# One layer with 32 routed experts on one core: TensorE reads an item's two table words inside the item ahead, and the body for one block comes first

## What is computed

```python
def expert_block(args):
    e, tok, gt = args
    xb = xf[tok]
    gu = xb @ w_gu[e] + b_gu[e]
    gate, up = gu[:, :D_EXPERT], gu[:, D_EXPERT:]
    gate = jnp.minimum(gate, SWIGLU_LIMIT)
    up = jnp.clip(up, -SWIGLU_LIMIT, SWIGLU_LIMIT)
    h = (up + 1.0) * gate * jax.nn.sigmoid(SWIGLU_ALPHA * gate)
    y = h @ w_down[e] + b_down[e]
    return y * gt[:, None].astype(y.dtype)
```

## Time and profile before

| | us |
|---|---|
| median of 3 runs | 2352.89 (2351.8 to 2353.47) |
| the profiled execution | 2354.07 |
| its span, first to last instruction | 2352.3 |
| PE busy | 2243.4 (95%) |
| DVE busy | 1712.5 (73%) |
| ACT busy | 1341.7 (57%) |

### The profile page before, as it was taken

One profiled execution on the slowest core, in us unless ns is written; L12 is line 12 of the kernel. 1 busy time (PEld: TensorE's weight loads), 2 busy tenths in 40 slices (PEclk: granted clock), 3 DMA queues, 4 the chain that ended last, 5 costly groups with the idle time before them and its releaser, 6 DMA issues.

```text
span 2352.3 us, 35229 instructions
## 1 busy us (share of the span) xinstructions
PE 2243.4 (95%) x10483; PEld 1658.5 (71%) x10484; DVE 1712.5 (73%) x2828; ACT 1341.7 (57%) x1785; POOL 359.4 (15%) x231
## 2 busy tenths in 40 slices
PE   8999998889999999999999999999999999999992
PEld 3544446667755678877787877878787787887872
DVE  0387794745445667778978799787979979778797
ACT  0368723555312555656766577566757757556575
POOL 0000941200020210101201031021103103101030
PEclk9999998989999999999999999999999999999996
DMA  4100002000322967688988799797979979768795
GB/s 179 72 5 36 1 0 92 1 1 1 135 79 99 279 212 233 229 307 291 339 300 303 238 328 370 230 324 236 373 232 335 365 231 343 284 230 307 231 335 216
DMA packets 83741, 494.13 MB, mean 210 GB/s; under 512 B 13342, under 2 KB 14622, under 8 KB 32580
## 3 DMA queue, kind: packets, MB, share of 16 engines
q1 hardware_dynamic: 69408, 451.24, 52.3%
q0 software_dynamic: 12592, 38.82, 6.8%
q10 hardware_dynamic: 1686, 3.38, 0.4%
HBM read 462.97 MB, written 38.01 MB: 213 GB/s over the span
## 4 chain that ended last, share of the span: by engine, by line
PE 76%; DVE 9%; issue 8%; ACT 5%; DVEq 1%; DMA 1%; ACTq 0%; POOL 0%; POOLq 0%; SPq 0%
PE ps L912 10%; PE ps L910 10%; PE ps L911 10%; PE ps L581 6%; PE ps L907 6%; PE ps L908 6%; PE ps L592 5%; PE ps L772 5%; DVE wlo L1630 3%; ACT whi L1158 2%; PE ps L755 2%; PE ps L920 2%; PE ps L736 2%; PE ps L875 1%; PE ps L743 1%
## 5 line engine op out<-in xcount | busy, mean ns | idle before, releaser
L1630 DVE TENSOR_TENSOR wlo<-raw,whi 128x2048 fp32r<-128x2048 f32 x388 | 886.1, 2288 | 244.5 <-ACT whi L1158 207.8
L1158 ACT ACTIVATE whi<-raw 128x2048 fp32r<-128x2048 f32 x388 | 743.2, 1916 | 327.4 <-PE ps L912 326.2
L911 PE MATMUL ps<-wlo,xhi 128*128 128x512 f32 x1024 | 398.8, 389 | 0.0
L912 PE MATMUL ps<-whi,xlo 128*128 128x512 f32 x1024 | 398.8, 389 | 0.0
L910 PE MATMUL ps<-whi,xhi 128*128 128x512 f32 x1024 | 398.7, 389 | 0.0
L1963 POOL DMA_INDIRECT acc<-ysb,idx_cur x45 | 87.5, 1945 | 959.5 <-DVE ysb L1797 584.4
L912 PEld LDWEIGHTS ps<-whi,xlo 128*128 128x128 f32 x1024 | 192.3, 188 | 40.3
L911 PEld LDWEIGHTS ps<-wlo,xhi 128*128 128x128 f32 x1024 | 192.2, 188 | 40.1
L910 PEld LDWEIGHTS ps<-whi,xhi 128*128 128x128 f32 x1024 | 192.3, 188 | 38.9
L910 PE MATMUL ps<-whi,hhi 128*128 128x512 f32 x512 | 206.5, 403 | 0.0
L912 PE MATMUL ps<-whi,hlo 128*128 128x512 f32 x512 | 200.4, 391 | 0.0
(11 more groups left out here) (340 smaller groups left out, 3346.9 us busy)
## 6 DMA issues: line engine op xcount, KB each, us to landing
raw<-in_w_gu SPq DMA_DIRECT2D x260, 1024.0 KB, 6.8
raw<-in_w_dn SPq DMA_DIRECT2D x128, 1024.0 KB, 5.6
raw<-in_w_out SPq DMA_DIRECT2D x2, 2048.0 KB, 12.5
h1all<-in_x SPq DMA_DIRECT2D x4, 1024.0 KB, 8.5
hext<-h1all SPq DMA_DIRECT2D x8, 512.0 KB, 3.1
acc<-h1all SPq DMA_DIRECT2D x8, 512.0 KB, 3.8
fin<-acc SPq DMA_DIRECT2D x4, 1024.0 KB, 8.3
out<-fin SPq DMA_DIRECT2D x8, 512.0 KB, 2.6
```

The source lines that it names most:

```text
L911: pe.matmul(bank_ap, hi, wlo[slot][:, col, :], start=False, stop=False)
L912: return pe.matmul(bank_ap, lo, whi[slot][:, col, :], start=False, stop=stop)
L1158: act.activation(whi[j % 2][:, 4 * g:4 * g + 4, :], raw[:, (j + 2) % 3, 4 * g:4 * g + 4, :], ACT.Copy)\
L1630: dve.tensor_tensor(wlo[j % 2][:, s, :], raw[:, (j + 2) % 3, s, :], whi[j % 2][:, s, :].bitcast(f32), ALU.subtract).then_inc(lo_done, 1)
```

## The change

Three things change, all on PE. The helper `load_entries` reads the two words into two registers that last over the turns, without the bounds check that `entry` makes; it is called once ahead of the loop for item 0, and in every item between `gate_up(1)` and `gate_up(2)` for the item after. The head of a turn only copies the two registers. And the body for one block stands ahead of the body for two.

```diff
-            entry = item_table(pe)
 ...
+            next_b1, next_n1 = pe.alloc_register("next_b1"), pe.alloc_register("next_n1")
+
+            def load_entries(i):
+
+                pe.reg_load(next_b1, table[0:1, bass.ds(i + MAX_ITEMS, 1)])
+                pe.reg_load(next_n1, table[0:1, bass.ds(i + 2 * MAX_ITEMS, 1)])
+
             def item(i, n1, blocks):
                 gate_up(0, i, n1, blocks)
                 find_slots(i + 1, fills_before(i, 0) + 1)
                 gate_up(1, i, n1, blocks)
+                load_entries(i + 1)
                 gate_up(2, i, n1, blocks)
 ...
             pe.wait_ge(tail_const, 8)
+            load_entries(0)
             with pe.Fori(0, n_items) as i:
-                b1, n1 = entry(1, i, 1), entry(2, i, MAX_ITEMS)
+                b1 = pe.snap(next_b1, min_val=0, max_val=1)
+                n1 = pe.snap(next_n1, min_val=0, max_val=MAX_ITEMS)
+                with pe.If(b1 < 1):
+                    item(i, n1, (0,))
                 with pe.If(b1 > 0):
                     item(i, n1, (1, 0))
-                with pe.If(b1 < 1):
-                    item(i, n1, (0,))
```

## The result

The changed kernel takes 2340.94 us, median of 4 runs (2335.43 to 2342.44), beside 2353.18 for the kernel before (4 runs, 2351.8 to 2353.99). The ratio is 0.994, 95% interval 0.9927 to 0.9952. It is faster, by 12.2 us; 2342.2 was forecast.

What follows compares the result with a forecast made beforehand. PE, busy 95% of the span, was taken as the bound, with DVE next in one-block items. Removing 18 border stalls wins 8.5 + 2.2 = 10.7 us, giving 2342.2 us; the 8-in-10 range was 2336 to 2350.

Steps and rivals of the forecast that it cites:

- The stalls' cause: Behind one-block items PE's sequencer needs about 2.65 us at the border, queued matmuls cover 1.67; moving two reads ends 18 stalls.
- The price of a read, 0.7 us: Each table read with its register work at PE's loop head was taken to cost 0.7 us, from DVE's border.
- The mid-item reads at 0: Two reads between quarters 1 and 2 cost 0, hidden behind twelve queued matmuls, 2.7 us of cover against 1.4.
- From one block to two: 9 x 0.94 = 8.5 us: Nine borders into two-block items each win 0.72 us of stall and 0.22 of pipeline refill, 8.5 us in all.
- the refill: A two-block item without a stall ahead need not refill the pipeline and runs 0.22 us shorter, 59.97 against 60.19.
- From one block to one: 9 x 0.24 = 2.2 us: Of the 0.98 us stall, 0.74 returns as PE waits for DVE's chain at `turn_h(3)`; 0.24 stays, nine times.
- The first turn at 0: The stall at the first item's end moves ahead of item 0 and costs the same: 0, bounds -5 to +3.5 us.
- The sum: 8.5 + 2.2 = 10.7 us won over the whole kernel, giving 2342.2 us against 2352.89, -0.45%.
- Cheap reads: Rival, 15%: PE's border is jumps and register work; at 0.25 us a read, stalls into two blocks stay, 2350.7 us.
- The gain used up: Rival, 12%: another chain of one-block items, or a second 3.5 us code stall in the first turn, leaves 2350 us.
- A stop in mid-item: Rival, 7%: the mid-item reads stop the array, 0.7 us in each of 32 items, slower at 2364.6 us.
- No give-back: Rival, 8%: DVE's border catches up and one-block items win the whole 0.98 + 0.2 us; 19.1 us won, 2333.8.

Runs made afterwards that it cites:

- reads_only: The changed kernel with the bounds check kept and the two-block body put first again, PE's reads still in mid-item: 2340.51 us, ratio 0.9944 to the kernel before.
- order_only: The kernel before with only the two bodies exchanged, PE's reads left at the loop's head: 2356.31 us, ratio 1.0011.
- head_reads_live: The kernel before with four more bounds-checked table reads at PE's loop head, which stay in the program: 2436.0 us in one run beside 2353.54.
- mid_reads_live: guarded with six more bounds-checked table reads in mid-item on PE, eight in all, which stay in the program: 2414.78 us in one run beside 2353.54.
- dve_ahead: guarded with DVE's four table reads also moved ahead, one behind each of four wlo splits of an item: 2329.95 us, ratio 0.990 to the kernel before.
- head_reads: The kernel before with four more reads at PE's loop head into an unused register, which the compiled program leaves out: 2352.14 us in one run.
- dve_only: The kernel before with DVE's four reads moved ahead and PE's left at its head: 2349.45 us beside 2353.83, ratio 0.9976.
- guarded: The changed kernel with the bounds check on PE's mid-item reads kept, and a register move added: 2340.93 us, ratio 0.9944 to the kernel before.
- mid_reads: guarded with six more mid-item reads on PE into an unused register, which the compiled program leaves out: 2340.75 us in one run.

## Why the prediction was right, step by step

**The stalls' cause.** Right. The reads' move alone ended all 18 (reads_only), the exchange of bodies none (order_only).

**The price of a read, 0.7 us.** Measured 0.64 (head_reads_live). Needed were 0.61 from one block to two, and the prediction called that close. It was closer than it sounded: 1.29 taken out against 1.28 to be taken. That these nine stalls went whole, and not all but a few hundredths, is in part luck. The price of a jump with its compare, 0.25, measured 0.28 (order_only). Its 2.40 us into a two-block item begin at this row, which the earlier trace rows do not show, and end at 1193.97:

```profile
1191.56 0.44 PE L888 MATMUL ps<-consts,xg_all 128*128 128x128 f32 x2 [0.23 <-DVE xlo L1748]
```

**The mid-item reads at 0.** Right, and the cover of 2.7 us was near: an estimated 3.4 in most items, 1.9 to 2.8 in one-block items behind two blocks (mid_reads_live). Eight reads, an estimated 5.15 us, were more than it could hide, and showed 1.7 to 3.3 us. That the queue is deep was taken from the border behind a two-block item, an estimated 2.9 us of work without a gap. How deep it is no run shows, for a wait of PE can end the cover first; the measured cover decides.

**From one block to two: 9 x 0.94 = 8.5 us.** Measured 9 x 0.82 = 7.4. The gap's part was right (0.72). The part for the refill was set at 0.22 from one pair of items; the 1018.86 item of the earlier trace rows, 59.96 to its last matmul, is the longest of nine whose mean is 59.90. Over all nine it is 0.10. The mean of the nine, against 59.75 for an item without a stall, would have given 0.15, and 7.8 us in all.

**From one block to one: 9 x 0.24 = 2.2 us.** The mechanism was right: of a gap of 0.97 most is given back to DVE's chain, and `turn_h(3)` came at +27.54 in the item laid out above, for +27.49. The step named one of the chain's two places only: in that item more of the delay is taken at `turn_h(2)` (0.53 us over the usual distance) than at `turn_h(3)` (0.27). The items vary, 37.29 to 38.19 to their last matmul where 37.79 was forecast, with a mean of 37.69. That makes 3.0 us. dve_ahead showed the cause: with DVE's four reads out of its border, L875 no longer waits, and these items are 36.90 long. What makes one such item 0.9 us longer than another is not shown.

**The first turn at 0.** Wrong by 2.0 us in the profiled execution. It was taken that the stall, the 3.71 us at item 0's end, moves ahead of item 0 and costs the same. No run shows this 0 or its bounds of -5 and +3.5, which were the author's estimates; before the change the stall and the eight matmuls behind it, starting 0.20 further apart than usual at a granted clock of 0.51, come to 5.1 us (3.5 + 1.6), and 2.0 of them were won. The stall moved into item 0, between its two blocks' quarter 0, and from item 0's start to item 2's the loop took 2.6 us less. Of that, 1.1 us is a shorter stall (2.62 for 3.71) and 1.6 the eight matmuls at half the clock that no longer follow it. In the table "half" counts the matmuls of the stretch that start about 0.43 apart, at a granted clock of 0.50 or 0.51 where a stretch of such alone was read (793 to 799 us in reads_only, 858.7 to 862 before; it is 1.00 from 795.7 to 799 us in the changed kernel, where they start 0.23 apart), and "stall" is the longest distance between two starts:

| profiled execution | PE's reads | body first | item 0's start to item 2's, us | stall | half |
|---|---|---|---|---|---|
| before | head | two-block | 125.30 | 3.71 | 8 |
| head_reads (the same program) | head | two-block | 125.21 | 3.52 | 8 |
| dve_only | head | two-block | 126.79 | 3.56 | 16 |
| order_only | head | one-block | 122.24 | 2.34 | 0 |
| reads_only | mid-item | two-block | 124.93 | 2.07 | 14 |
| after | mid-item | one-block | 122.67 | 2.62 | 0 |
| guarded | mid-item | one-block | 122.71 | 1.38 | 7 |
| mid_reads (guarded again) | mid-item | one-block | 123.04 | 1.61 | 7 |
| dve_ahead | mid-item | one-block | 123.24 | 1.67 | 7 |

The body order is shown to set where the stall falls: at item 0's end with the two-block body first, inside item 0 with the other. With the reads at the head the exchange also shortens the stretch, by 3.0 to 4.6 us, in one execution against three. With the reads in mid-item the stretch is 1.7 to 2.3 us shorter, but that is not shown to come from the order: in reads_only the 14 matmuls at half the clock, an estimated 2.8 us (14 x 0.20), stand at item 0's start, far ahead of the stall, and without them its stretch is no longer than the others. In guarded, mid_reads and dve_ahead the seven slow matmuls come just ahead of the stall, which is then shorter than in the changed kernel. Why the stall's length changes, and what decides between the two clock levels here, is open: the start of item 0 itself lies between 790.7 and 795.9 us from one profiled execution to the next, and the fetches were not varied by themselves.

**The sum.** 10.7 us were forecast and 11.6 measured between the profiled executions, 12.2 between the medians. The terms are 7.4 for 8.5, 3.0 for 2.2, 2.0 for 0, and -0.7 behind the last matmul, which no step spoke of and which was not followed up. So the sum is nearer than its parts, which is luck: the first turn made up for the refill.

**The two parts of the change.** The exchange of bodies, which the forecast took as neutral in the first turn and dear by two jumps, is worth nothing that the runs can tell once the reads are gone (reads_only 2340.51, guarded 2340.93), and costs 2.4 us with the reads in place (order_only). All of the win that the runs can tell comes from the reads.

**The rivals.** Cheap reads: excluded, 0.64. The gain used up: excluded; with DVE's reads moved, one-block items run 0.6 to 0.8 us shorter than after the change, so the DMA queues do not hold them at that length, and the code stall did not double. A stop in mid-item: excluded for two reads, present for eight. No give-back: excluded in this kernel, and true of dve_ahead, where DVE's border has caught up. It forecast 19.1 us, and there from item 2 to the last matmul 23.7 are won, 6.0 of them in the items behind two blocks, which had no stall on PE at all.

## What to carry to other kernels

Two table reads at the head of this loop cost nothing where what was queued behind the last wait outlasted the whole border (0.23 from start to start behind two-block items), and stood in gaps of 0.95 and 1.20 where it did not; so price the border (reads at 0.64 us and jumps at 0.28 here) against the queued matmuls, kind of item by kind of item, for a single number can hide that one kind has next to no room. Moving the reads off the engine that stalled won only up to the next engine's border: PE's alone gave 13.0 us, DVE's alone 4.4 to 5.6, both 24.0, so the same edit belongs on every engine of the chain at once. An experiment that adds work to price it has to be looked up in the compiled program first, since here the loads without a user were left out of it (35229 instructions with and without them).

## What was not expected of the hardware

- A wait hid in an engine that shows no stall. One-block items behind two-block items had no gap ahead in the kernel before (0.23) and still lost 0.60 us each, 6 us in all, to DVE's reads.
- Eight reads, an estimated 5.15 us, in mid-item held the next matmul up by 1.7 us in most items and by up to 3.3 in others, so the sequencer's lead over the array was an estimated 1.9 to 3.4 us there. Which wait sets it was not isolated.
- The stall of the first turn, with one instruction fetch of 0.02 MB beside it, was 3.71 us (3.56 and 3.52 in other profiled executions with that loop), 2.07 with the reads moved. With the bodies exchanged it was inside item 0, 2.6 us in the changed kernel, 2.3 in order_only and 1.4 to 1.7 in the three others, from start to start. A fetch alone is no stall: two more of that size, at 811 and 834 us in the kernel before, have PE's matmuls 0.23 apart around the first and no gap over 0.4 around the second. From 960 to 2300 us the DMA queues show no instruction fetch at all. That the stall is a wait for this fetch is argued from its place, and not shown.
- Behind some idle times of about 3.1 to 3.4 us at the borders (head_reads_live), though not behind most, the first matmuls started 0.43 us apart instead of 0.23 (at a granted clock of 0.50 from 1211.5 to 1215 us), and the mean granted clock of the execution fell from 0.981 to 0.974. In mid_reads_live the same followed an idle time of 2.22 us at 1570.8 us (granted clock 0.50 in the 3.2 us behind it) and did not follow one of 3.09 us at 1391.6 us (1.00), so here the length of the idle time alone did not decide it.
